# Squared feed-forward, stick-breaking and linear attention: another order of work at the ends of stages

## The reference

```python
def squared_relu_mlp(xn, w_up, w_down):
    return jnp.square(jax.nn.relu(xn @ w_up)) @ w_down

def third_block(x, norm_gains, ...):
    h = x
    for i in range(DEPTH_3):                       # 4 layers, kind = i % 3
        xn = rms_norm(h, norm_gains[i, 0])
        m = ...  # stick_breaking_mixer, short_conv_mixer or gla_mixer of xn
        h = h + rms_norm(m, norm_gains[i, 1])
        f = squared_relu_mlp(rms_norm(h, norm_gains[i, 2]), ffn_w_up[i], ffn_w_down[i])
        h = h + rms_norm(f, norm_gains[i, 3])
    return h
```

## Time and profile before

| what | value |
|---|---|
| median of 3 runs | 2749.66 us (2747.09 to 2750.38) |
| the profiled run | 2748.72 us |
| its span, first to last instruction | 2746.9 us |
| third block | from about 1590 us to the end |
| PE busy in the span | 98% |
| DVE, ACT, POOL busy | 68%, 45%, 23% |
| granted TensorE clock | 0.993 of full speed over the span |

### The profile page before, as it was taken

How to read it: one execution, slowest core, us unless ns; L and a number is a source line. 1 busy time by engine, 2 the same in 40 slices (tenths; PEclk the granted TensorE clock), 3 DMA queues, 4 the chain that set the end, 5 groups by cost and what they waited for, 6 DMA issues and landing times.

```text
span 2746.9 us, 43616 instructions
## 1 busy us (share of the span) xinstructions
PE 2691.2 (98%) x17237; PEld 2387.7 (87%) x17237; DVE 1876.3 (68%) x2061; ACT 1244.9 (45%) x1594; POOL 630.3 (23%) x519
## 2 busy tenths in 40 slices
PE   8999999999999999999999999999999999999998
PEld 8988799999879999997899888888888878888887
DVE  6887765588778886665766657666766667665765
ACT  4444544444454444444444444344534454435442
POOL 5863300089437860001100100000000420000000
PEclk9999999999999999999999999999999999999999
DMA  8765055567437766533455425535643445433552
GB/s 299 257 215 167 30 192 196 193 247 270 173 106 263 273 213 234 188 126 113 161 197 188 160 98 222 195 126 191 237 183 123 155 154 229 184 131 108 220 201 92
DMA packets 127002, 502.05 MB, mean 183 GB/s; under 512 B 11168, under 2 KB 12480, under 8 KB 93488
## 3 DMA queue, kind: packets, MB, share of 16 engines
q1 hardware_dynamic: 112768, 450.40, 45.6%
q0 software_dynamic: 14128, 50.18, 5.3%
HBM read 499.48 MB, written 1.06 MB: 182 GB/s over the span
## 4 chain that ended last, share of the span: by engine, by line
PE 89%; DVE 6%; ACT 2%; issue 2%; DMA 1%; POOL 0%; DVEq 0%; SPq 0%; ACTq 0%; POOLq 0%
PE duo L1274 8%; PE duo L1259 8%; PE duo L1260 8%; PE duo L1404 7%; PE duo L1257 7%; PE duo L1408 7%; PE duo L1412 7%; PE duo L1273 4%; PE duo L1776 4%; PE duo L1781 4%; PE duo L1777 4%; DVE in_lo L373 2%; PE duo L2324 1%; PE duo L2325 1%; PE duo L2326 1%
## 5 line engine op out<-in xcount | busy, mean ns | idle before, releaser
L373 DVE TENSOR_TENSOR in_lo<-ring_in,in_hi 128x2048 fp32r<-128x2048 f32 x295 | 691.9, 2346 | 336.7 <-ACT in_hi L366 336.5
L366 ACT CAST in_hi<-ring_in 128x2048 fp32r<-128x2048 f32 (+1 forms) x293 | 556.0, 1898 | 239.0 <-PE duo L1781 125.5
L373 DVE TENSOR_TENSOR down_lo<-ring_down,down_hi 128x1024 fp32r<-128x1024 f32 (+1 forms) x196 | 347.8, 1774 | 28.5 <-ACT down_hi L366 28.5
L1521 ACT CAST hid_hi<-act 128x256 fp32r<-128x256 f32 (+1 forms) x196 | 93.4, 476 | 418.9 <-DVE act L1607 348.5
L366 ACT CAST down_hi<-ring_down 128x1024 fp32r<-128x1024 f32 (+1 forms) x196 | 260.5, 1329 | 43.6 <-PE duo L1412 43.6
L1404 PE MATMUL duo<-down_hi,hid_hi 128*128 128x512 f32 x928 | 242.7, 393 | 6.2 <-ACT hid_hi L1521 6.1
L1257 PE MATMUL duo<-feat,in_hi 128*128 128x512 f32 x1024 | 246.6, 392 | 0.0
L1259 PE MATMUL duo<-feat,in_hi 128*128 128x256 f32 (+1 forms) x1015 | 240.3, 280 | 3.6 <-ACT in_hi L366 3.5
L1408 PE MATMUL duo<-down_lo,hid_hi 128*128 128x512 f32 x928 | 239.4, 390 | 0.0
L1260 PE MATMUL duo<-feat,in_hi 128*128 128x256 f32 x1015 | 238.9, 279 | 0.0
L1412 PE MATMUL duo<-down_hi,hid_lo 128*128 128x512 f32 x928 | 238.9, 389 | 0.0
(11 more groups left out here) (537 smaller groups left out, 5561.7 us busy)
## 6 DMA issues: line engine op xcount, KB each, us to landing
ring_in<-in_ffn_in SPq DMA_DIRECT2D x196, 1024.0 KB, 6.7
ring_down<-in_ffn_down SPq DMA_DIRECT2D x132, 512.0 KB, 3.8
ring_down<-in_ffn_down SPq DMA_DIRECT2D x64, 1024.0 KB, 4.9
mod_w<-in_w_ada POOLq DMA_DIRECT2D x72, 512.0 KB, 5.3
ring_in<-in_sb_w_qkv SPq DMA_DIRECT2D x24, 1024.0 KB, 5.1
ring_in<-in_conv_w_in SPq DMA_DIRECT2D x12, 1024.0 KB, 5.1
ring_in<-in_gla_w_in SPq DMA_DIRECT2D x12, 1024.0 KB, 5.1
ring_in<-in_nsa_w_in SPq DMA_DIRECT2D x10, 1024.0 KB, 5.2
```

Of the source, the lines that this page charges most:

```text
L366: act.copy(hi[:, s, 0:n], raw[:, s, 0:n]).then_inc(hi_ready.sem, 1)
L373: dve.tensor_tensor(lo[:, s, 0:n], raw[:, s, 0:n], hi[:, s, 0:n].bitcast(F32), ALU.subtract).then_inc(lo_ready.sem, 1)
```

## The change

- The first unit of each squared feed-forward has its own order on DVE (`_open_squared`): sum and square first, then `down_lo`, then `hid_lo`. Where the feed stands behind a `PostNorm`, both halves of the squares are made on ACT (`squares_alone`; seven feeds).
- `_vector_by_part`: behind a `Linear`, the first diagonal and both of the first rows come ahead of the second mean, and the second diagonal ahead of the last row; behind a feed-forward, the means and the diagonals keep their place and part precedes row.
- Stick-breaking start: PE's step 2 no longer waits for the last read of q and k, and DVE makes the softplus of pair 1 ahead of that read.
- Stick-breaking end: at step 8 PE makes the first tile of the output matrix ahead of the sums of the last pair; the tile is kept in bank 4.
- Linear attention, start: 16 high products of the second weight piece ahead of the wait for its low part; the two small loads are issued from the `Feed` ahead of its squares; the two buffers are cleared by two ACT copies of 128x1024 instead of POOL.
- Linear attention, end: ACT's second silu ahead of its last `in_hi`; DVE's `in_lo` of the same piece behind `lo` of the third head; PE makes all four values, then three turns, the first tile of the output, then the fourth turn; ACT squares all four before any high feature; DVE's order is written out.

```diff
@@ -596,13 +596,14 @@
...
+        self.squares_alone = isinstance(before, PostNorm)
@@ -684,7 +685,11 @@
     def squares_act(self, act):
         k = self.k
         self.feeds.wait_x(act, 3)
-        act.activation(k.y[:, 0, :], k.x[:, 0, :], ACT.Square, accum_out=k.stat("squares", 0, 1)).then_inc(k.squares_ready.sem, 1)
+        last = act.activation(k.y[:, 0, :], k.x[:, 0, :], ACT.Square, accum_out=k.stat("squares", 0, 1))
+        if self.squares_alone:
+            self.feeds.wait_x(act, 4)
+            last = act.activation(k.y[:, 1, :], k.x[:, 1, :], ACT.Square, accum_out=k.stat("squares", 1, 1))
+        last.then_inc(k.squares_ready.sem, 1)
...
+        if self.squares_alone:
+            return
@@ -1093,18 +1101,24 @@
...
+        from_rows = isinstance(self.feeds, Linear)
         for t in range(TT):
             dve.wait_ge(k.acc_squared.sem, self.sq0 + t + 1)
-            self._times_row(dve, t)
             self._part(dve, t)
+            if not from_rows:
+                self._times_row(dve, t)
         dve.wait_ge(k.acc_squared.sem, self.sq0 + 3)
         self._mean(dve, 0)
-        self._times_row(dve, 2)
+        if from_rows:
+            self._times_row(dve, 0)
+            self._times_row(dve, 1)
+            self._diagonal(dve, 0)
         dve.wait_ge(k.acc_squared.sem, self.sq0 + 4)
         self._mean(dve, 1)
+        self._times_row(dve, 2)
+        for t in range(int(from_rows), TT):
+            self._diagonal(dve, t)
...
-        for t in range(TT):
-            self._diagonal(dve, t)
         for c in range(4):
...
-        unit(0, 0, False)
+        if opening:
+            opening(eng)
+        else:
+            unit(0, 0, False)
...
     def _square(self, dve, m, j):
+        self._square_sum(dve, m, j)
+        self._square_low(dve, m, j)
+
+    def _open_squared(self, dve):
+
+        self._square_sum(dve, 0, 0)
+        self._down_lo(dve, 0, 0)
+        self._square_low(dve, 0, 0)
@@ -1675,7 +1707,8 @@
...
-        self.begun = isinstance(before, Attention) and not isinstance(before, HybridAttention)
+        self.near = isinstance(before, Attention) and not isinstance(before, HybridAttention)
+        self.begun = self.near or isinstance(before, StickBreaking)
         if self.begun:
             before.out = self
...
     def acc(self, t, b):
         lo, hi = self.blocks[b]
-        if self.begun and b == 0:
+        if self.near and b == 0:
             return self.k.bank[t][:, 0:hi - lo]
...
+                    if b == 0 and isinstance(self.feeds, GlaOut):
+                        self.feeds.last_turn(pe)
                     if b == 0 and self.feeds.turns_late:
...
+            self.out.tile(pe, 0, 0, 0)
         if 1 <= step <= n:
             pe.wait_ge(k.sb_softplus.sem, self.sp0 + step)
...
             self._values(pe, step - 2)
 
     def tensor(self, pe):
-        wait_all(pe, self.before)
+        k, proj = self.k, self.feeds
+        pe.wait_ge(k.acc_read_act.sem, proj.ra0 + 2)
         for step in range(self.EARLY, self.n + 2):
+            if step <= self.EARLY + 1:
+                pe.wait_ge(k.acc_read_dve.sem, proj.rd0 + 9 + step - self.EARLY)
             self.step_tensor(pe, step)
@@ -2266,7 +2307,7 @@
 
     def step_vector(self, dve, step):
         k, n = self.k, self.n
-        if self.EARLY <= step <= n:
@@ -2384,6 +2425,8 @@
                 rows = self.rrow.unsqueeze(1).broadcast_to([P, 2, TOKENS])
                 for i in range(2):
                     c = lo // P + 2 * i
+                    if (b, i) == (5, 1):
+                        self.sb.softplus(dve, 1)
...
         k, at = core, 0
+        before.early_loads = self._loads
+        self.downs = core.down_units
@@ -4409,19 +4454,29 @@
...
-            pe.wait_ge(k.in_lo_ready.sem, g + 1)
...
+            ahead = 2 * int(b == 0 and h == 1)
+            if ahead:
+                pe.wait_ge(k.in_hi_ready.sem, g + 1)
+            for j in range(ahead):
+                for c in range(4):
+                    if j == 0:
+                        feat_wait(pe, self, 4 * h + c)
+                    pe.matmul(outs[j], w_hi[:, c, mine[j]], self.feat_hi[:, 4 * h + c, :], start=False, stop=False, skip_group_check=True)
+                    pe.matmul(outs[j], w_hi[:, c, mine[j]], self.feat_lo[:, 4 * h + c, :], start=False, stop=False, skip_group_check=True)
+            pe.wait_ge(k.in_lo_ready.sem, g + 1)
...
     def scalar(self, act):
         k, u = self.k, self.u0
         in_hi(k, act, u + 2)
+        zeros = k.c("causal", 0, P).unsqueeze(1).broadcast_to([P, 8, P])
+        for i in range(2):
+            act.copy(self.kf[i].rearrange("p (a n) -> p a n", n=P), zeros).then_inc(self.cleared, 1)
...
         self._evict(act, 0, 5)
         self.out.silu(act, 0)
         self._evict(act, 1, 5)
+        self.out.silu(act, 1)
         in_hi(k, act, u + 13)
...
-                in_lo(k, dve, u + 2 * b + 7)
+                if b < 3:
+                    in_lo(k, dve, u + 2 * b + 7)
...
-    def gpsimd(self, pool):
-        k = self.k
-        wait_all(pool, self.feeds.before)
+    def _loads(self, pool):
+
+        k = self.k
+        pool.wait_ge(k.down_used.sem, self.downs)
         pool.dma_start(self.w_low.rearrange("p (c n) -> p c n", c=KC), self.w[:, 3 * D:3 * D + 16].rearrange("(c p) n -> p c n", p=P)).then_inc(self.landed, 16)
         pool.dma_start(self.w_up[0:16, :], k.dram["gla_w_gate_up_3"]).then_inc(self.landed, 16)
-        for i in range(2):
-            pool.memset(self.kf[i], 0.0).then_inc(self.cleared, 1)
+
+    def gpsimd(self, pool):
+        k = self.k
...
     def tensor(self, pe):
         pe.wait_ge(self.feeds.merged, 8)
-        for step in range(6):
-            if step < 4:
-                self._values(pe, step)
-            if step >= 2:
-                self._turn(pe, step - 2)
+        for h in range(4):
+            self._values(pe, h)
+        for h in range(3):
+            self._turn(pe, h)
@@ -4720,17 +4785,14 @@
 
     def scalar(self, act):
         k = self.k
-        self.silu(act, 1)
-        for step in range(7):
...
+        for h in range(4):
+            act.wait_ge(self.valued, self.valued0 + h + 1)
...
+        for h in range(4):
+            self._hi(act, h)
...
+        self._mean(dve, 0)
+        self._mean(dve, 1)
+        self._scale(dve, 0)
+        self._mean(dve, 2)
+        self._scale(dve, 1)
+        self._mean(dve, 3)
+        self._scale(dve, 2)
+        self._lo(dve, 0)
+        self._scale(dve, 3)
+        self._lo(dve, 1)
+        self._lo(dve, 2)
+        in_lo(self.k, dve, self.feeds.u0 + 13)
+        self._lo(dve, 3)
```

## The result

The changed kernel takes 2730.02 us at the median of four runs (2726.35 to 2730.89), the kernel before 2749.65 us (2747.09 to 2750.38). The ratio is 0.9925, with a 95% interval of 0.9911 to 0.9938. The interval of the ratio reaches from 2725.2 to 2732.6 us, so well into the range. In five further runs of a second comparison the ratio was 0.9918 (0.9905 to 0.9932): 22.5 us.

What follows compares the result with a forecast made beforehand. TensorE, busy 98% of the span, was taken as the bound; 6.7 + 1.6 + 2.0 + 2.2 + 1.7 + 2.4 = 16.6 us off 2748.72, plus 0.94 to the median, gave 2733.0 us, range 2729.5 to 2739.5.

Steps and rivals of the forecast that it cites:

- the range: Foretold span of the measured time, 2729.5 to 2739.5 us, given a chance of about 0.84.
- What bounds the kernel: TensorE, busy 98%; its third-block waits, 17.4 us, are what can go; clock granted in full, nothing from it.
- A: First unit of the four squared networks: PE's wait for `hid_hi` goes, 1.67 us a site, 6.7 in all (6.1 to 7.1).
- The spare of 0.7: First unit of the squared networks: the reordered chain ends at 1670.5, PE arrives at 1671.2, 0.7 us to spare.
- The price of the second square: Squared networks: ACT's second square, about 1.1 us ahead of `down_hi`, beside 5.2 us idle, costs nothing.
- B: Norms behind a Linear, four sites: PE waits less for the diagonals, 0.4 us a site, 1.6 (0.6 to 1.9).
- C and D: Stick-breaking, two starts and two ends: waits for last q/k read and last softplus go, 2.0 and 2.2 us.
- E: Linear attention start: PE's waits for `in_lo` and `before_r` go, 1.7 us (0.8 to 2.0).
- the 0.3 taken off: Linear attention start: first small load's issue may delay the norm's second diagonal by up to 0.7 us; 0.3 deducted.
- F: Linear attention end: PE's 4.1 us wait for scaled values shrinks, gain 2.4 us (1.2 to 3.5).
- The slide of the loads: Squared networks: ring loads start some 1.8 us later, land after 6.7 to 7.7 us, leaving 5.6 us.
- rivals 1 to 4: Mixer waits re-form, 2738.1, 0.15; feed order useless, 2739.8, 0.05; nothing measurable, 2744 to 2755, 0.06; late loads, about 2757 us, 0.03.

## Why the prediction was right, and where it fell short

- **What bounds the kernel.** Right: PE's waits in the third block were the whole gain there, and 15.3 of 17.7 us went.
- **A.** 1.67 a site foretold, 1.66 measured alone. The spare of 0.7 was 0.85. The price of the second square was rightly nothing. At these four sites its gain was nothing as well, which the prediction didn't say.
- **B.** 1.7 for 1.6.
- **C and D.** 4.0 for 4.2.
- **E.** 1.9 for 1.7; the 0.3 taken off for the load beside the norm's diagonal was not due.
- **F.** 2.4 for 2.4, by other waits than foretold; 0.4 of it A brings as well, at a wait that the prediction counted for F alone.
- **The slide of the loads.** As foretold, and the slack covered it.

So rivals 1 to 4 did not come about. That F came to the foretold number, with its wait in other pieces, is in part luck.

**The step that failed is the first part's**: "the clock was granted in full there [...] so nothing is to be had from it". The row showed it for one execution. Over nine traces the clock fell in five, behind the very waits that F takes away. The same holds for the earlier trace rows: 1.18 us was one of two values, and the other is 3.43. Both make the kernel before longer, on average, than the trace on which the sum was made: by 5/9 of 1.5 us, and by 0.6 us at the diagonals (1.3 and 2.9 longer in two of six traces, 0.2 to 0.3 shorter in three). Worked out like this, the gain is 16.5 + 0.8 + 0.6 = 17.9 us, of which the prediction's sum lacked 1.4.

These 1.4 us alone do not put the result outside the range: a gain of 17.9 would be 2731.8 us. It lies within the interval of the first comparison (17.0 to 24.5 us), 0.8 us below that of the second (18.7 to 26.1), and at the lower edge of that of all runs together (17.9 to 22.6). The medians say 19.6 and 21.2. Where the rest of the 20.6 us comes from, and whether these further 2 to 3 us are real, is open: no trace shows them in the third block, the first 1590 us vary by 8.6 us with no order by kernel, and nine runs of the changed kernel are too few to tell 2 us from none.

The second fault was the range, and it is this that the measured 2729.0 crossed, by 0.5 us. Its lower end was the sum of bounds "less 1 for the runs' own spread", from three runs that lay within 3.3 us. Sixteen runs lay within 12.6, and 23 within 17.7. And the range was set about the median, as if three runs fixed it.

## What to carry to other kernels

A sum over waits of one trace gives what the change does to that trace, here to 0.2 us. Ahead of a forecast of the time, ask of each wait that goes what else it costs in other executions: whether the clock may fall behind it, and whether a long time beside another engine's work is one value of several. Take the spread of single runs from more than three of them. Look also at what GpSimd does while VectorE is on the path to TensorE: here the clearing of two buffers held VectorE up, and moved to ScalarE, with the loads issued earlier, it held up nobody.

## What the runs showed of the hardware

- With waits of TensorE of 1.4, 1.5 to 1.8 and 0.9 us within some 7 us, the clock went to its lower level, 1.2 GHz, in five of nine executions, for some 3 us and at a price of 1.3 to 1.6 us. With 4.8, 1.1 and 0.5 us in their place, it stood there for over 12 us in the one execution that was profiled, at 5 us.
- A `tensor_scalar` of 128x128 on VectorE took 0.28 us alone. The first of two took 1.84 beside GpSimd's clearing of two 128x1024 buffers, and with two small loads issued ahead of the clearing 1.12 in four executions and 3.36 in two.
